# Retention groups of a streaming encoder: half swaps of q and k as transfers inside SBUF, and the first value tiles projected block by block

## The reference

```
def rotary(x, pos):
    ...
    x1, x2 = xf[..., :half], xf[..., half:]
    return jnp.concatenate([x1 * cos - x2 * sin, x2 * cos + x1 * sin], axis=-1)
```

```
a = einsum(q, k) * d_intra
o = einsum(a, v) + einsum(q * d_q, s)
s = s * d_c + einsum(k * d_k, v)
```

## Time and profile before

| | us |
|---|---|
| median of 3 runs | 3080.16 (3079.82 to 3083.72) |
| profiled execution | 3077.81 |
| its span | 3076.0 |
| TensorE busy | 2929.1 (95%) |
| VectorE, ScalarE, GpSimd busy | 1134.9, 1012.8, 809.6 |

### The profile page before, as it was taken

How to read it: one execution, slowest core, us unless ns; L and a number is a source line. 1 busy time by engine, 2 the same in 40 slices (tenths; PEclk the granted TensorE clock), 3 DMA queues, 4 the chain that set the end, 5 groups by cost and what they waited for, 6 DMA issues and landing times. The chain is left out here.

```text
span 3076.0 us, 55523 instructions
## 1 busy us (share of the span) xinstructions
PE 2929.1 (95%) x24012; PEld 2676.0 (87%) x24012; DVE 1134.9 (37%) x2548; ACT 1012.8 (33%) x1820; POOL 809.6 (26%) x528
## 2 busy tenths in 40 slices
PE   6999999999999999999979999999999999999996
PEld 4989888888888898999968898888888898899995
DVE  3411234334534543255133213334353543532631
ACT  3221423323434544222041233323334544532201
POOL 1212222222323323332222222212223413333320
PEclk8999999999999999999989999999999999999998
DMA  6121233233212211253232112212211221223323
GB/s 230 58 76 37 99 113 118 92 112 116 59 51 57 61 48 57 94 182 103 88 121 70 67 49 92 93 51 78 85 46 57 61 68 37 75 84 144 131 95 145
DMA packets 109954, 269.37 MB, mean 88 GB/s; under 512 B 38992, under 2 KB 45264, under 8 KB 108688
## 3 DMA queue, kind: packets, MB, share of 16 engines
q1 hardware_dynamic: 109712, 265.83, 25.6%
HBM read 208.20 MB, written 57.60 MB: 86 GB/s over the span
## 5 line engine op out<-in xcount | busy, mean ns | idle before, releaser
L283 PE MATMUL ps<-sb_h_split,sb_w_split 128*128 128x364 f32 (+1 forms) x3264 | 1157.7, 355 | 8.1 <-POOL sb_w_split L340 4.2
L284 PE MATMUL ps<-sb_h_split,sb_w_split 128*128 128x364 f32 (+1 forms) x3264 | 1072.4, 329 | 1.4 <-issue 1.4
L285 PE MATMUL ps<-sb_h_split,sb_w_split 128*128 128x364 f32 (+1 forms) x3264 | 1072.5, 329 | 0.0
L283 PEld LDWEIGHTS ps<-sb_h_split,sb_w_split 128*128 128x128 f32 x3264 | 616.8, 189 | 67.4 <-issue 38.7
L284 PEld LDWEIGHTS ps<-sb_h_split,sb_w_split 128*128 128x128 f32 x3264 | 616.9, 189 | 7.3
L338 POOL CAST sb_w_split<-sb_w_raw 128x1024 fp32r<-128x1024 f32 x152 | 164.5, 1082 | 1742.7 <-PE ps L285 1454.3
L285 PEld LDWEIGHTS ps<-sb_h_split,sb_w_split 128*128 128x128 f32 x3264 | 614.2, 188 | 1.5 <-issue 1.5
L340 POOL TENSOR_TENSOR sb_w_split<-sb_w_raw,sb_w_split 128x1024 fp32r<-128x1024 f32 x152 | 367.3, 2417 | 12.2
L1392 DVE COPY sb_fox<-ps 128x512 f32<-128x512 f32 (+3 forms) x208 | 109.1, 542 | 283.2 <-PE ps L1265 282.7
L325 ACT ACTIVATE sb_raw_qk<-ps 128x364 f32<-128x364 f32 (+2 forms) x176 | 64.6, 394 | 332.7 <-PE ps L285 332.6
L1331 ACT ACTIVATE sb_fox<-sb_fox 128x128 f32<-128x128 f32 (+5 forms) x144 | 111.2, 772 | 114.0 <-DVE sb_fox L1370 113.8
(11 more groups left out here) (275 smaller groups left out, 4382.1 us busy)
## 6 DMA issues: line engine op xcount, KB each, us to landing
sb_w_raw<-in_wblk SPq DMA_DIRECT2D x154, 512.0 KB, 5.6
sb_ada_fox<-in_adaw SPq DMA_DIRECT2D x32, 512.0 KB, 4.3
sb_raw_qk<-scratch_gate SPq DMA_DIRECT2D x24, 544.0 KB, 3.6
sb_fox<-scratch_fcum SPq DMA_DIRECT2D x8, 1600.0 KB, 7.2
sb_w_raw<-in_wbr SPq DMA_DIRECT2D x48, 256.0 KB, 4.1
scratch_gate<-sb_fox SPq DMA_DIRECT2D x16, 544.0 KB, 7.8
scratch_gate<-sb_delta SPq DMA_DIRECT2D x16, 544.0 KB, 4.5
sb_h_split<-scratch_o SPq DMA_DIRECT2D x16, 544.0 KB, 10.4
```

The source lines that it names most:

```text
L283: pe.matmul(out, w_hi, x_hi, start=first, stop=False)
L284: pe.matmul(out, w_hi, x_lo, start=False, stop=False)
L285: return pe.matmul(out, w_lo, x_hi, start=False, stop=last)
```

## The change

SyncE issues, ahead of the parameter loads, sixteen transfers inside SBUF: for q and for k, four row groups of 32 partitions, each in two pieces (1024 columns and 64), from `raw_qk` to the partner rows of `swapped`. `swapped` lies in slab 12 (q) and slab 7 (k). The six swap matmuls go, and with them their PSUM entries; the ring's later entries are renumbered by 6. VectorE waits for the eight transfers of a tensor (`swap_loaded`, 128) and multiplies `swapped` by sin in one instruction, SBUF to SBUF.

TensorE starts the phase with the value projection. The first two entries (four token tiles) are projected one weight block at a time, 128 columns a matmul: first the block that is ready (`half` g), then, after the wait for the second, the other. They go to banks 1 and 2 (`vbank`). The last three entries stay at 256 columns, in banks 7, 5 and 6. In group 1 the wait for ScalarE's end of the phase before stands ahead of these.

```diff
+            swap_loaded = [sem(f"swap_loaded_{x}") for x in "qk"]
...
-                cos, sin, tmp, Kd = slab(4)[:, 0:TOK], slab(5)[:, 0:TOK], slab(6), slab(7)
+                cos, sin, Kd = slab(4)[:, 0:TOK], slab(5)[:, 0:TOK], slab(7)
...
+                swapped = [slab(12)[:, 0:TOK], slab(7)[:, 0:TOK]]
...
-                OUT, NORM = [[18, 19, 20], [21, 25, 26]], [22, 27]
-                owners = (["dve"] * 15 + [(state_ready, 4), (state_ready, 8), (state_ready, 9)]
+                OUT, NORM = [[12, 13, 14], [15, 19, 20]], [16, 21]
+                owners = (["dve"] * 9 + [(state_ready, 4), (state_ready, 8), (state_ready, 9)]
...
+                def vbank(e):
+
+                    return 1 + e if e < 2 else B0 + e % NB
+
                 @block.sync
                 def _(sp):
                     enter(sp, "sp", nr)
+                    for x in range(2):
+                        for i in range(0, P, B):
+                            o = i + B if i % (2 * B) == 0 else i - B
+                            for u, a, w in PIECES:
+                                sp.dma_start(swapped[x][i:i + B, a:a + w], raw_qk[o:o + B, x, u:u + w])\
+                                    .then_inc(swap_loaded[x], 16)
                     sp.dma_start(cos, A["rot"][:, 0, :]).then_inc(params_loaded, 16)
...
-                    def swap_halves(n):
-
-                        x, s = divmod(n, 3)
-                        u, w = RAW[s]
-                        ring.acquire(pe, n)
-                        pe.matmul(ps[:, ring.bank(n), 0:w], swap, raw_qk[:, x, u:u + w],
-                                  start=True, stop=True).then_inc(bank_ready, 1)
-
-                    for m in range(5):
-                        if m == 3 and g:
-                            pe.wait_ge(done["act"], nr)
-                        swap_halves(m)
+                    def values(e, half=None):
+
+                        t, c = VN[e]
+                        for j in range(c):
+
+                            a = (t + j) * P if t + j < 8 else TOK - P
+                            to = ps[:, vbank(e), 256 * j:256 * j + 256]
+                            for k in range(KC):
+                                if half is None:
+                                    mm = three(pe, to, hs[:, 0, k, a:a + P], hs[:, 1, k, a:a + P],
+                                               ws[:, 0:2, 0, k, :], ws[:, 0:2, 1, k, :], k == 0, k == KC - 1)
+                                else:
+                                    mm = three(pe, to[:, P * half:P * half + P],
+                                               hs[:, 0, k, a:a + P], hs[:, 1, k, a:a + P],
+                                               ws[:, half, 0, k, :], ws[:, half, 1, k, :], k == 0, k == KC - 1)
+                        return mm
+
+                    await_split(pe, L, first)
+                    for e in range(2):
+                        values(e, g)
                     await_split(pe, L, first + 1)
-                    for e, (t, c) in enumerate(VN):
...
+                    for e in range(2):
+                        values(e, 1 - g).then_inc(proj_done, 1)
+                    if g:
+                        pe.wait_ge(done["act"], nr)
+                    for e in range(2, len(VN)):
+                        values(e).then_inc(proj_done, 1)
                     fill = blocks(pe, L, [(3 * b - 1, first + b) for b in range(2, RET_N)], B0, NB)
                     pe.wait_ge(normed, 2)
+                    pe.wait_ge(evacuated, 2)
...
                     for x, dst in enumerate((q, k_)):
-                        for s, (a, w) in enumerate(STREAMS):
-                            dve.wait_ge(bank_ready, 1 + 3 * x + s)
-                            dve.tensor_tensor(tmp[:, a:a + w], ps[:, ring.bank(3 * x + s), 0:w],
-                                              sin[:, a:a + w], ALU.mult).then_inc(dve_took, 1)
+                        dve.wait_ge(swap_loaded[x], 128)
+                        link(dve.tensor_tensor(swapped[x], swapped[x], sin, ALU.mult))
                         for u, a, w in PIECES:
                             link(dve.tensor_tensor(dst[:, a:a + w], raw_qk[:, x, u:u + w], cos[:, a:a + w],
                                                    ALU.mult))
-                        dve.wait_ge(dve_took, 3 * (x + 1))
-                        dve.tensor_tensor(dst[:, 0:TOK], dst[:, 0:TOK], tmp[:, 0:TOK], ALU.add)\
+                        dve.tensor_tensor(dst[:, 0:TOK], dst[:, 0:TOK], swapped[x], ALU.add)\
                             .then_inc(normed, 1)
```

More of the change, by code:

```diff
@@ L863, in _ @@
-                    await_split(pe, L, first + 1)
-                    for e, (t, c) in enumerate(VN):
-                        if e >= NB:
-                            pe.wait_ge(evacuated, e - NB + 1)
+                    def values(e, half=None):
+                        t, c = VN[e]
                         for j in range(c):
                             a = (t + j) * P if t + j < 8 else TOK - P
+                            to = ps[:, vbank(e), 256 * j:256 * j + 256]
                             for k in range(KC):
[L871 to L876, removed]
+                                if half is None:
[6 more added lines that the diff above has]
+                        return mm
@@ L877, in _ @@
+                    await_split(pe, L, first)
+                    for e in range(2):
+                        values(e, g)
+                    await_split(pe, L, first + 1)
+                    for e in range(2):
[4 more added lines that the diff above has]
+                        values(e).then_inc(proj_done, 1)
                     fill = blocks(pe, L, [(3 * b - 1, first + b) for b in range(2, RET_N)], B0, NB)
@@ L878, in _ @@
                     pe.wait_ge(normed, 2)
+                    pe.wait_ge(evacuated, 2)
                     for n, (t, c) in enumerate(G3):
-                        ring.acquire(pe, 6 + n)
+                        ring.acquire(pe, n)
                         for j in range(c):
-                            mm = pe.transpose(ps[:, ring.bank(6 + n), P * j:P * j + P],
+                            mm = pe.transpose(ps[:, ring.bank(n), P * j:P * j + P],
                                               Q4(k_)[:, t + j, :], ident)
@@ L885, in _ @@
                     for n, (t, c) in enumerate(G3):
-                        e = 9 + 2 * n
+                        e = 3 + 2 * n
                         ring.acquire(pe, e)
@@ L896, in _ @@
                         turns(fill, 12)
-                    pe.wait_ge(dve_took, 9)
+                    pe.wait_ge(dve_took, 3)
                     pe.wait_ge(evacuated, 5)
@@ L900, in _ @@
                     for n, (t, c) in enumerate(G3):
-                        ring.acquire(pe, 15 + n)
+                        ring.acquire(pe, 9 + n)
                         for j in range(c):
                             for h in range(2):
-                                mm = pe.matmul(ps[64 * h:64 * h + 64, ring.bank(15 + n), P * j:P * j + P],
+                                mm = pe.matmul(ps[64 * h:64 * h + 64, ring.bank(9 + n), P * j:P * j + P],
                                                Q4(Kd)[:, t + j, 64 * h:64 * h + 64],
@@ L928, in norm_sum @@
                                   start=True, stop=True).then_inc(bank_ready, 1)
-                    pe.wait_ge(dve_took, 15)
+                    pe.wait_ge(dve_took, 9)
                     pe.wait_ge(conv_done, 1)
@@ L958, in _ @@
                         act.activation(V[0:P - lo, t:t + c, :],
-                                       ps[lo:P, B0 + e % NB, 0:256 * c].rearrange("p (t c) -> p t c", t=c),
+                                       ps[lo:P, vbank(e), 0:256 * c].rearrange("p (t c) -> p t c", t=c),
                                        ACT.Copy).then_inc(evacuated, 1)
@@ L1048, in _ @@
                     for n, (t, c) in enumerate(G3):
-                        dve.wait_ge(bank_ready, 7 + n)
+                        dve.wait_ge(bank_ready, 1 + n)
                         col = kd[:, 0:P] if t < 8 else kd[:, P:2 * P]
-                        dve.tensor_tensor(Q4(Kd)[:, t:t + c, :], Q4(ps[:, ring.bank(6 + n), 0:P * c]),
+                        dve.tensor_tensor(Q4(Kd)[:, t:t + c, :], Q4(ps[:, ring.bank(n), 0:P * c]),
                                           col.unsqueeze(1).to_broadcast([P, c, P]), ALU.mult)\
@@ L1055, in _ @@
                         for h in range(2):
-                            e = 9 + 2 * n + h
+                            e = 3 + 2 * n + h
                             dve.wait_ge(bank_ready, e + 1)
@@ L1063, in _ @@
                     for t in range(NTILE):
-                        n = 15 + t // 4
+                        n = 9 + t // 4
                         dve.wait_ge(bank_ready, n + 1)
```

## The result

| | before | after |
|---|---|---|
| median (lowest to highest), us | 3079.99 (3077.88 to 3083.72), 4 executions | 3131.45 (3125.22 to 3137.96), 4 executions |
| profiled execution | 3077.8 | 3137.96 (span 3136.2) |

The ratio is 1.0166 with a 95% interval of 1.0143 to 1.0189: slower by 51 us, where 21 were forecast, and above the range. The direction was right, the size was not.

What follows compares the result with a forecast made beforehand. TensorE, busy 95% of the span, was taken to bound the kernel. Group changes of +5.8, +4.1, +7.4 and +4.1 us summed to +21.4, giving 3101.6 us against the median; own range 3094 to 3108, with rivals 3080 to 3113.

Steps and rivals of the forecast that it cites:

- Part 1: Swaps leave TensorE, removing about 3.5 us of swaps a group and another 2 us of waits in group 1.
- Part 2: Value stage: 192 matmuls of 128 columns at 0.111 us replace 96 of 256 at 0.119, 9.9 us more a group.
- B: Value stage: narrow fp32r matmuls fall to the fp32 pace, 0.22 us each; +98.6 us, 3179 us; chance 0.12.
- Part 3: SyncE's queue: sixteen issues at 0.467 us ahead of the parameter loads, so VectorE starts 7.5 us later.
- Twice the row: SyncE's queue: upper bound for an issue, twice the 0.467 us read from the profile; kernel then 3113 us.
- Part 4: VectorE's rotation: one SBUF product at 1.29 us, cos 1.48, add 1.29; 8.3 us for two tensors.
- The sum: Four groups in order: +5.8, +4.1, +7.4 and +4.1 us, together +21.4; 3101.6 us against the median.
- The wait for k: TensorE waits for the rotated k in layer 1 group 0 alone, some 6 us.
- A: Value stage: columns set the pace, 0.060 us a narrow matmul; 3079 us; chance 0.13 including the strip up to the forecast.
- C: SyncE's queue: swaps land late, issues at twice the price or SBUF copies slower than loads; 3113 us; chance 0.12.

Runs made afterwards that it cites:

- run 2: Kernel before with the first two entries projected by 128-column halves, swaps kept on TensorE ahead of them; 3113.84 us, ratio 1.0105.
- run 5: Changed kernel with only its first 24 of 192 narrow matmuls streaming their block twice, 256 columns; 3107.6 us, ratio 1.0086.
- run 3: Changed kernel with each of the 192 narrow matmuls streaming its block twice, 256 columns; 3112.72 us, ratio 1.0103.
- run 6: Changed kernel with the wait for the second block's split moved ahead of the narrow stream in every group; 3190.62 us, ratio 1.0352.
- run 8: Changed kernel with tables loaded first, four swap transfers for sixteen, one token tile by halves at 256 columns, the others whole; 3093.11 us, ratio 1.0038.
- run 4: Changed kernel with only the first token tile projected block by block, 48 narrow matmuls; 3105.96 us, ratio 1.0077.
- run 1: Changed kernel with all value tiles 256 columns wide again, both splits waited for first, swaps still transfers; 3104.0 us, ratio 1.0075.
- run 7: Kernel before with group 1's sixth swap one entry later and VectorE waiting for the two tables alone; 3074.05 us, ratio 0.9974.

## Why the prediction was wrong, point by point

**Part 1 (swaps removed): right in size, and it missed what else they did.** The stage starts where the swaps started, and the waits of 0.75 and 1.24 us are gone. But the swaps also stood between the stand-still and the value stream. In run 2, where they still do, the clock holds; without them, and with the narrow stream first, it doesn't.

**Part 2 (192 narrow matmuls): this is the step that failed.** The price of 0.111 us was right to the digit: 0.111 in the rows of 103.48 to 103.59, groups 1 +4.4 and +4.5 for +4.1, run 5's 168 in 18.71 us. What failed is that the price was read from rows at a granted clock of 1.00 and taken for the whole stage. In groups 0 it held for 2.6 us; then each cost 0.213, and the low level added 19.3 us a group. None of the rivals had it: B, at 0.22 a matmul, has the size of the slow stretches but a false reason (two records a matmul) and all four groups. Runs 2, 3, 5 and 6 show the cause: a narrow stream right behind a stand-still. The executions without a profile bear it out: their mean clock is 0.986 to 0.989 in runs 2, 3 and 5 and 0.960 to 0.962 in run 6, against 0.976 to 0.981 in the changed kernel and 0.985 to 0.989 in the runs of before.

**Part 3 (SyncE): the term was too small.** 0.63 to 0.71 us an issue (10.07 to 11.38 us for sixteen) for 0.467; from SyncE's first issue to VectorE's first product it is 17.4 us (130.79 - 113.36), in run 5 18.1, where it was 6.4 before (layer 1 group 0, 1628.17 to 1634.59): 11 to 12 us later, not 7.5. Twice the row, the upper bound, was not reached by any of these issues, though.

**Part 4 (VectorE): right.** 1.29, 1.49 and 1.29 for a tensor, 8.3 in all where GpSimd is idle.

**The sum.** With the clock at 2.4 GHz (run 5) the groups 0 take 40.9 and 54.3 us, +6.3 and +14.8 for the forecast +5.8 and +7.4, and the kernel 3107.6 us: inside the forecast's own range. The wait for k then stands in layer 1 group 0 alone, as forecast, but is 12.7 us and not 6: the stretched rotation (13.9 us under the split, 11.2 forecast) comes on top of the late issues. In the changed kernel that wait is not seen at all. There the slow stage hides it, and the clock's net price in layer 1 group 0 is only 60.2 - 54.3 = 5.9 us, in layer 0 group 0 60.0 - 40.9 = 19.1; together 25, against 23.9 between the medians of the two kernels and 25.3 when each is taken against its own runs of before. From the forecast of 21.4 to the 60.1 of the profiled execution: 25.0 for the clock, 7.4 for the late k of layer 1 group 0, 1.2 in the three other groups, 5.1 outside the groups.

**Rivals.** A (columns set the pace) is refuted at either level: at 2.4 GHz 0.111 for 128 columns and 0.119 for 256, at 1.2 GHz 0.213 for both. C had the mechanism that stretched layer 1 group 0, at 1.5 times the issue's row in place of twice.

**Open.** Why 2.6 us appear before the first gate matmul in the changed kernel (0 to 0.5 in those that keep the swaps, 1.1 to 2.6 in those with transfers) was not tested, nor what lengthens the profiled executions outside the groups by up to 8.4 us (run 8; 7.7 in run 4, 6.1 in run 2). Nor is it settled what decides whether a stand-still of about 1 us brings the clock down (run 4, groups 1), or how long it stays down (the spread of the changed kernel).

## What to carry to other kernels

Before taking a wide stretch of work away from TensorE, look at what it stands behind: work that looks like overhead can be what keeps the clock up after a stand-still. Price narrow matmuls by the weight-load cadence, and read the granted clock window by window, since a stage at half clock shows as busy time and not as a wait. A transfer costs its issue too; sixteen ahead of a load that VectorE needs are 11 us on that load.

## What the runs showed of the hardware

- A stream of 128-column fp32r matmuls without a gap did not bring TensorE back from 1.2 to 2.4 GHz in 36.1 us (changed kernel) nor in 40.8 (run 6); 256-column streams did in 3.1 to 5.3 us (changed kernel, runs 1, 4 and 6). The Trainium skill, "TensorE: Matmul & The Clock Gate", section "Loop structure matters more than you think", says that matmuls kept back to back stay at the high clock. Here they were back to back and stayed at the low one, until they were wide.
- A stand-still of 0.71 to 0.87 us was followed by the low level where 128-column matmuls came next (changed kernel, run 4, groups 0), and not where 256-column ones (runs 3, 5 and 8) or 512-column ones (before, runs 2 and 7) did; one of 3.67 us was followed by it with either (runs 1 and 6).
- At 1.2 GHz a 128-column and a 256-column matmul with its load both take 0.213 us from start to start.
- A copy of 32 partitions inside SBUF costs the issuing queue 0.63 to 0.71 us, one with two runs a row (run 8) 1.11.
- Beside GpSimd's split, VectorE's add of two SBUF tiles takes 3.45 us in place of 1.29 (run 5), as before the change.
